# Each expert form's code split in two blocks: a short opening behind the comparisons and a rest reached by a hinted jump

## The chip, the cores and the metric

One core of one Trainium2 chip runs the kernel. The metric is the device time of one execution in microseconds (us). The profile takes one execution; it shows the engines PE (TensorE), its weight loads (PEld), DVE (VectorE), ACT (ScalarE), POOL (GpSimd) and SP (the engine that issues most transfers), and, under names with a q (PEldq, ACTq, DVEq), the instructions that an engine's sequencer handles itself: branches, register work, waits.

## The reference, cut to what matters

Two layers of a hybrid encoder: each has a token mixer, and after it a channel mixer, which is a dense SwiGLU in the first layer and a top-2-of-8 expert SwiGLU in the second. The expert part is what the change touches:

```
logits = t @ w_router + b_router              # t: 256 tokens x 1024
top_val, top_idx = top_k(logits, 2)
gates = softmax(top_val)
for each expert e, on the tokens routed to it:
    y_e = (silu(x @ w_gate_e[e]) * (x @ w_up_e[e])) @ w_down_e[e]     # 1024 -> 3584 -> 1024
out = sum over a token's two experts of gate * y_e
```

All is float32. An expert has 3 x 1024 x 3584 weights, 44 MB; the eight together are 352 MB of the 483 MB that the kernel reads.

## The kernel before

The program runs the mixer, the dense layer, the second mixer and the routing as straight code, and then a loop over the eight experts. How many tokens an expert gets is known only at run time (`cnt`), so each of PE, ACT and DVE holds the code of one expert six times, in six forms for up to 32, 64, 128, 160, 192 or 256 tokens (`NVAR`). POOL and SP run one loop body for all forms.

`experts(eng, name, emit)` (L618 to L649) writes this loop for one engine. A block `next` (L629, L630) adds one to the expert number and ends the loop after the eighth; `pick` (L632, L633) loads the token count from SBUF; a chain of comparisons (L641 for the forms under 128, L643 for those over it) jumps to the form. The six forms follow in the order 128, 32, 64, 160, 192, 256. Each begins with a branch hint (L646), which names the jump at the form's end (L648) and its target `next`. Only the form of 128 stands right behind the comparisons: the others lie behind it, 192 for instance some 7,500 PE instructions further on. A form's length in PE instructions is about 1,150 for 128, 2,360 for 32, 1,290 for 64, 2,670 for 160 and 2,440 for 192 (a matrix product of a rounded type is a weight load and a multiply, a float32 one two of each, and a transpose one of each).

An expert is 14 stages over the inner width. A stage takes two units of gate and up weights (halves of the 1024 rows, 1 MB each) and one unit of down weights. SP loads the units in order (L749) into a ring of 14 slots, and each of its loads waits until PE has finished with the slot's last unit, told by `gu_full` for a stage's gate and up product and by `down_done`.

- Forms 32 and 64 (`expert_whole`) multiply float32 directly. On PE, `gate_up(s)` (L1278) runs two stages ahead of `down(s)` (L1290); `turn` (L1264) transposes the activated product in between. ACT does `silu` of a stage, DVE the product `gated` (L2235) and a copy (L2257).
- Forms 128 and 256 (`expert_split`, L1388, L1419) and 160 and 192 (`expert_wide`, L1322, L1328, L1341, L1350) split each unit into a rounded high part (ACT, `weights_hi`, about 1.9 us) and a low part (DVE, `weights_lo`, L2241, about 2.3 us), and PE multiplies the parts. The inputs are split too (`h_parts`, DVE, L2268 and L2270, or L2311 and L2314).
- Before the first product of an expert PE waits for `xe` (the gathered tokens, copied by POOL, L2436, once the expert before has done its last gate and up product), and in the split forms for DVE's split of it and ACT's first high part.
- At an expert's end ACT and DVE copy the output from PSUM (`hT`), ACT issues its store, and all go back to `next`.

Of the kernel before, what the change touches and what calls it, by code (L numbers as in the profile page):

```python
# [281 lines left out]
def build(nc, ap, out, ypairs):  # L282
# [13 lines left out]
    with ExitStack() as ctx:  # L296
# [321 lines left out]
        def experts(eng, name, emit, first_variant=128):  # L618
# [25 lines left out]
            for n in sorted(NVAR, key=lambda n: n != first_variant):  # L644
                with nc.body(label(n), valid_engines=own):
                    back = eng.mark_branch_hint_location()  # L646
                    emit(eng.snap(turn, min_val=0, max_val=NE - 1), n)
                    eng.br(label("next")).branch_hint(back)  # L648
# [133 lines left out]
        def _(pe):  # L782
# [484 lines left out]
            def expert_whole(e, n):  # L1267

                def gate_up(s):

                    w = [landed_unit(e, "gu", s, h).rearrange("p (k c) -> p k c", k=KD // 2) for h in range(2)]
                    if s >= 2:
                        pe.wait_ge(act_ready, at_unit(e, n, s - 2))
                    bank = PG[:, s % 2, :]
                    width = gate_up_of(n, s)[3]
                    for k in range(KD):
                        for i in range(P // n):
                            last = mm(bank[i * n:(i + 1) * n, 0:width], xe[:, k, 0:n],  # L1278
                                      w[k // 4][:, k % 4, i * width:(i + 1) * width], start=(k == 0), stop=(k == KD - 1))
                    last.then_inc(gu_full, 2)  # L1280
# [12 lines left out]

                for i in range(STAGES + 2):
                    if i < STAGES:
                        gate_up(i)
# [12 lines left out]
            def expert_wide(e, n):  # L1309
# [54 lines left out]
                pe.wait_ge(x_split, e * 4 + 4)  # L1364
                for s in range(STAGES + 1):
                    if s < STAGES:
                        if s:
                            pe.wait_ge(act_ready, e * FT + FT + 2 * s - 1)
                        gate_up_half(s, 0)
# [8 lines left out]
            def expert_split(e, n):  # L1378
# [14 lines left out]

                def gate_up(s):
# [5 lines left out]
                    for h in range(2):  # L1400
                        q = expert_at["gu", s, h]
                        hi_ready(e, q)
                        if s == 0 and h == 0:
                            pe.wait_ge(x_split, e * 4 + 2)
                        gate_up_part(s, h, x_hi, w_hi_e[q % HI], opens=(h == 0))
                        if s == 0 and h == 0:
                            pe.wait_ge(x_split, e * 4 + 4)
                        gate_up_part(s, h, x_lo, w_hi_e[q % HI]).then_inc(hi_used, 1)
# [27 lines left out]

                for s in range(STAGES + 1):
# [8 lines left out]
            def expert(e, n):  # L1446
                pe.wait_ge(xe_ready, e + 1)
                (expert_whole if n < P else expert_split if n % P == 0 else expert_wide)(e, n)
# [18 lines left out]
        def _(act_e):  # L1467
# [224 lines left out]

            def silu(e, n, u, m):
# [22 lines left out]
            def expert_whole(e, n):  # L1716
                for u, s, j, m in units(n):
                    silu(e, n, u, m)
                ae.sem_inc(conv_hi, USES)
# [3 lines left out]
            def expert_wide(e, n):  # L1723
# [12 lines left out]
                for q in range(HI):  # L1736
                    weights_hi(e, q)
# [10 lines left out]
            def expert_split(e, n):  # L1748
                bl = turns(n)
                done = HI + 1  # L1750
                for q in range(done):
                    weights_hi(e, q)
# [13 lines left out]
            def expert(e, n):  # L1766
                (expert_whole if n < P else expert_split if n % P == 0 else expert_wide)(e, n)
# [28 lines left out]
        def _(ve):  # L1796
# [462 lines left out]
            def expert_whole(e, n):  # L2259
                for u, s, j, m in units(n):  # L2260
                    gated(e, n, u, m)
                    turned_whole(e, n, u, m)
                ve.sem_inc(conv_lo, USES)
                ve.sem_inc(x_split, 4)

            def expert_wide(e, n):
                ve.wait_ge(xe_ready, e + 1)
                V.tensor_copy(h_parts[:, 0, :, 0:n], xe[:, :, 0:n]).then_inc(x_split, 2)  # L2268
                ve.wait_ge(x_split, e * 4 + 2)
                V.tensor_tensor(h_parts[:, 1, :, 0:n], xe[:, :, 0:n], h_parts[:, 0, :, 0:n].bitcast(F32),  # L2270
                                ALU.subtract).then_inc(x_split, 2)
# [21 lines left out]
                for q in range(HI):  # L2293
                    weights_lo(e, q)
# [12 lines left out]
            def expert_split(e, n):  # L2307
                bl = turns(n)
                ve.wait_ge(xe_ready, e + 1)
                for i, j, m in bl:  # L2310
                    V.tensor_copy(x_hi[j], xe[:, :, j * P:(j + 1) * P]).then_inc(x_split, 2 // len(bl))  # L2311
                ve.wait_ge(x_split, e * 4 + 2)
                for i, j, m in bl:
                    V.tensor_tensor(x_lo[j], xe[:, :, j * P:(j + 1) * P], x_hi[j].bitcast(F32),  # L2314
                                    ALU.subtract).then_inc(x_split, 2 // len(bl))
                done = HI + 1
                for q in range(done):
                    weights_lo(e, q)
# [12 lines left out]
            def expert(e, n):  # L2331
                (expert_whole if n < P else expert_split if n % P == 0 else expert_wide)(e, n)
# [138 lines left out]
```

## Time and profile before

| | |
|---|---|
| three timed runs | 1830.52, 1839.72, 1842.34 us (median 1839.72) |
| the profiled execution's own time | 1832.89 us |
| its span, first to last instruction | 1831.1 us |
| mean granted TensorE clock | 0.917 of full |
| PE busy | 1598.6 us, 87% |
| DMA | 488.94 MB, mean 267 GB/s |

With the inputs used here the eight experts take the forms 32, 32, 128, 64, 160, 32, 192 and 64; they are called expert 0 to 7. They begin at about 822 us and end at about 1804 us of the span. A row of the chain of waits gives where the chain that ended last stood: start, length, and the engine and line that it stood on, "issue" being time in which the engine waited for nothing that the profile shows.

### The profile page before, as it was taken

How to read it: one execution, taken by the hardware profiler on the slowest of the kernel's cores; microseconds unless marked ns; L12 is line 12 of the kernel's file. 1: busy time of each engine (PE TensorE's matmuls, PEld its weight loads, DVE VectorE, ACT ScalarE, POOL GpSimd, SP SyncE). 2: the span in 40 equal slices, each digit the busy share in tenths (PEclk: the TensorE clock that was granted, in tenths of full speed). 3: DMA queues.
4: the chain of work that ended last, by engine and by line, in shares of the span. 5: the costliest groups of instructions: out<-in, count | busy, mean ns of one | idle time of the engine just before them, and what ended most of it. 6: DMA issues, size and time to landing. Idle time of an engine off the chain costs nothing.

```text
span 1831.1 us, 30902 instructions
## 1 busy us (share of the span) xinstructions
PE 1598.6 (87%) x12644; PEld 1288.1 (70%) x12645; DVE 710.6 (39%) x1017; ACT 545.7 (30%) x749; POOL 63.2 (3%) x66
## 2 busy tenths in 40 slices
PE   5999997999999999967566799989998749999894
PEld 4777776999987687746344687548897538888552
DVE  2162115555532431140000787116665015666212
ACT  2122114343321321020000676115654015545201
POOL 0010000000000100010000000000000000000002
PEclk8998598999999986898787899999999879999998
DMA  9632255744534133268999999999667997555794
GB/s 364 258 111 97 92 190 206 306 187 170 198 103 188 58 128 137 93 253 362 424 424 425 425 411 389 407 424 377 267 249 278 387 422 327 230 207 230 284 424 167
DMA packets 74563, 488.94 MB, mean 267 GB/s; under 512 B 9792, under 2 KB 13920, under 8 KB 16544
## 3 DMA queue, kind: packets, MB, share of 16 engines
q1 hardware_dynamic: 72176, 479.94, 65.2%
q10 hardware_dynamic: 1648, 4.59, 0.7%
q8 instruction: 119, 1.95, 0.4%
q0 software_dynamic: 576, 2.10, 0.4%
q14 instruction: 44, 0.36, 0.1%
HBM read 482.66 MB, written 3.93 MB: 266 GB/s over the span
## 4 chain that ended last, share of the span: by engine, by line
PE 78%; DMA 9%; issue 4%; DVE 4%; ACT 2%; POOL 1%; SPq 1%; ACTq 0%; POOLq 0%; DVEq 0%
PE PG L1278 9%; DMA arena<-in_experts 5%; PE Y L905 5%; PE PG L1388 4%; PE PG L1322 4%; PE TRB L1322 4%; PE Y L1290 4%; PE Y L1350 4%; PE Y L913 3%; PE Y L1162 3%; PE PG L869 3%; PE PG L870 3%; PE PG L871 3%; DMA ring<-in_experts 3%; PE TRB L1328 3%
## 5 line engine op out<-in xcount | busy, mean ns | idle before, releaser
L1278 PE MATMUL PG<-ring,mixT 128*32 128x128 f32 (+1 forms) x1920 | 115.2, 345 | 63.3 <-issue 63.3
L1471 ACT ACTIVATE parts<-ring 128x2048 fp32r<-128x2048 f32 x84 | 158.5, 1906 | 12.4 <-PE Y L871 8.2
L1278 PEld LDWEIGHTS PG<-ring,mixT 128*32 128x32 f32 (+1 forms) x1920 | 88.6, 136 | 93.6 <-issue 77.9
L2257 DVE COPY arena<-TRB 128x64 f32<-128x64 f32 (+1 forms) x70 | 17.6, 251 | 338.7 <-PE TRB L1264 338.7
L1471 ACT ACTIVATE rope<-PG 64x128 f32<-64x128 f32 (+2 forms) x84 | 27.1, 324 | 376.1 <-PE PG L1278 351.7
L1278 PE MATMUL PG<-arena,mixT 128*32 128x128 f32 (+1 forms) x1664 | 100.3, 349 | 41.7 <-issue 41.7
L869 PE MATMUL PG<-h_parts,parts 128*128 128x256 f32 x448 | 127.5, 285 | 10.2 <-DVE parts L2133 10.2
L870 PE MATMUL PG<-h_parts,parts 128*128 128x256 f32 x448 | 127.3, 284 | 0.0
L871 PE MATMUL PG<-h_parts,parts 128*128 128x256 f32 x448 | 127.1, 284 | 0.0
L1278 PEld LDWEIGHTS PG<-arena,mixT 128*32 128x32 f32 (+1 forms) x1664 | 78.1, 138 | 68.6 <-issue 55.5
L2133 DVE TENSOR_TENSOR parts<-ring,parts 128x2048 fp32r<-128x2048 f32 x42 | 95.9, 2292 | 25.6 <-ACT parts L1471 25.6
L2241 DVE TENSOR_TENSOR ring_parts<-ring,parts 128x2048 fp32r<-128x2048 f32 x42 | 95.0, 2287 | 20.8 <-PE Y L1341 18.4
L2241 DVE TENSOR_TENSOR parts<-arena,parts 128x2048 fp32r<-128x2048 f32 x42 | 95.2, 2287 | 18.3 <-PE Y L1341 15.5
L905 PE MATMUL Y<-hT,ring 128*128 128x256 f32 x416 | 93.6, 385 | 0.0
L869 PEld LDWEIGHTS PG<-h_parts,parts 128*128 128x128 f32 x448 | 85.6, 191 | 10.8 <-DVE parts L2133 10.4
L905 PEld LDWEIGHTS Y<-hT,ring 128*128 128x128 f32 x416 | 79.4, 193 | 11.2
L870 PEld LDWEIGHTS PG<-h_parts,parts 128*128 128x128 f32 x448 | 85.7, 191 | 0.0
L871 PEld LDWEIGHTS PG<-h_parts,parts 128*128 128x128 f32 x448 | 85.6, 191 | 0.0
L1471 ACT ACTIVATE parts<-arena 128x2048 fp32r<-128x2048 f32 x42 | 78.9, 1902 | 3.8 <-PE PG L1388 3.8
L913 PE MATMUL Y<-ring,hT 128*128 128x256 f32 (+2 forms) x320 | 63.5, 363 | 2.8 <-ACT hT L1471 2.8
L871 PE MATMUL Y<-parts 128*128 128x256 f32 x224 | 63.4, 283 | 0.0
L870 PE MATMUL Y<-parts 128*128 128x256 f32 x224 | 63.4, 283 | 0.0
(375 smaller groups left out, 2909.4 us busy)
## 6 DMA issues: line engine op xcount, KB each, us to landing
ring<-in_experts SPq DMA_DIRECT2D x168, 1024.0 KB, 13.0
arena<-in_experts SPq DMA_DIRECT2D x168, 1024.0 KB, 16.4
ring<-in_weights SPq DMA_DIRECT2D x116, 1024.0 KB, 5.8
ring<-in_weights SPq DMA_DIRECT2D x4, 512.0 KB, 4.1
ypairs<-hT ACTq DMA_DIRECT2D x3, 512.0 KB, 5.3
tok<-in_x SPq DMA_DIRECT2D x1, 1024.0 KB, 8.8
result<-scr SPq DMA_DIRECT2D x2, 512.0 KB, 2.6
ring<-in_weights SPq DMA_DIRECT2D x2, 432.0 KB, 6.7
```

Of the source, the lines that this page charges most:

```text
L869: mm(out_, w_hi[w][:, c], x[0], start=first, stop=False, skip_group_check=True)
L870: mm(out_, w_hi[w][:, c], x[1], start=False, stop=False, skip_group_check=True)
L871: return mm(out_, w_lo[w][:, c], x[0], start=False, stop=last, skip_group_check=True)
L905: last = mm(bank_part, ring[:, s, k, c:c + m], hT[:, k, :], start=(k == 0), stop=(k == KD - 1))
L913: last = mm(bank_part, hT[:, k, b * P:(b + 1) * P], ring[:, s, k, 0:m], start=(k == 0), stop=(k == KD - 1))
L1278: last = mm(bank[i * n:(i + 1) * n, 0:width], xe[:, k, 0:n], w[k // 4][:, k % 4, i * width:(i + 1) * width], start=(k == 0), stop=(k == KD ...
L1290: last = mm(o, actT[:, s % 2, f, 0:n], w[:, f, c:c + width], start=(s == 0 and f == 0), stop=(s == STAGES - 1 and f == 1))
L1322: last = mm(both, hi[:, k, i // 2, i % 2, :], h_parts[:, :, h * KD // 2 + k, 0:n], start=(h == 0 and k == 0), stop=False, skip_group_check ...
L1350: last = mm(o, a[:, s % 2, f, :], w[:, f, c:c + width], start=(opens and s == 0 and f == 0), stop=(closes and s == STAGES - 1 and f == 1))
L1471: return nc.scalar.activation(out_, in_, func, **kw)
L2133: V.tensor_tensor(w_lo[d % SPLITS], ring[:, slot_of[slot_of_dense(d)], :, :].rearrange("p k c -> p (k c)"), w_hi[d % SPLITS].bitcast(F32), ...
L2241: V.tensor_tensor(w_lo_e[q % SLOTS_E], ring_e[q % SLOTS_E].rearrange("p k c -> p (k c)"), w_hi_e[q % HI].bitcast(F32), ALU.subtract).then_ ...
```

## The change

Each form is written as two blocks instead of one. Six openings stand right behind the comparisons, in the old order; then come six rests in the same order. An opening ends in a jump to its rest, and a hint for this jump is the opening's first instruction; the rest begins with the hint for the jump back to `next`, as the whole form did. The functions that write an engine's part of an expert take a flag `opening` and write one piece or the other. What an opening holds:

- PE: the wait for `xe`; for 32 and 64 the half of stage 0's gate and up product that uses the first unit (16 and 8 of 32 and 16 products); for 128 and 256 the two high-part products of the first unit; for 160 and 192 all products of the first unit.
- ACT: `silu` of stage 0 (32 and 64), or the first three (160 and 192) or four (128 and 256) `weights_hi`.
- DVE: `gated` and the copy of stage 0 (32 and 64), or the split of `xe` and the first three or four `weights_lo`.

In the forms of 160 and 192 ACT gets a Silu of a single element at the head of the rest, ahead of the fourth `weights_hi`. Six openings take 46 instructions on ACT, 76 on DVE and about 300 on PE.

```diff
-            for n in sorted(NVAR, key=lambda n: n != first_variant):
+            layout = sorted(NVAR, key=lambda n: n != first_variant)
+            for n in layout:
                 with nc.body(label(n), valid_engines=own):
+                    on = eng.mark_branch_hint_location()
+                    emit(eng.snap(turn, min_val=0, max_val=NE - 1), n, True)
+                    eng.br(label(f"rest_{n}")).branch_hint(on)
+            for n in layout:
+                with nc.body(label(f"rest_{n}"), valid_engines=own):
                     back = eng.mark_branch_hint_location()
-                    emit(eng.snap(turn, min_val=0, max_val=NE - 1), n)
+                    emit(eng.snap(turn, min_val=0, max_val=NE - 1), n, False)
                     eng.br(label("next")).branch_hint(back)
...
+                if opening:
+                    gate_up(0, [0])
+                    return
                 for i in range(STAGES + 2):
                     if i < STAGES:
-                        gate_up(i)
+                        gate_up(i, [0, 1] if i else [1])
...
-                pe.wait_ge(x_split, e * 4 + 4)
+                if opening:
+                    pe.wait_ge(x_split, e * 4 + 4)
+                    gate_up_half(0, 0)
+                    return
...
-            def expert(e, n):
-                pe.wait_ge(xe_ready, e + 1)
-                (expert_whole if n < P else expert_split if n % P == 0 else expert_wide)(e, n)
+            def expert(e, n, opening):
+                if opening:
+                    pe.wait_ge(xe_ready, e + 1)
+                (expert_whole if n < P else expert_split if n % P == 0 else expert_wide)(e, n, opening)
...
+            def silu_table():
+
+                run(rc[0:1, 0, 0:1], rc[0:1, 0, 0:1], ACT.Silu)
...
-                for q in range(HI):
-                    weights_hi(e, q)
+                if opening:
+                    for q in range(HI):
+                        weights_hi(e, q)
+                    return
+                silu_table()
```

On PE, the form of 32 stood behind the whole form of 128; its first rows before (ISA rows are register work or a wait, L1278 the gate and up product, L1264 the transpose):

```order
L646 BRANCH_PREFETCH_HINT
L647 ISA
L1250 ISA
L1278 MATMUL PG<-ring,mixT 32x128 x64
L1255 ISA
```

And now, the openings of 128 and 32 (here L1403 is the product that was L1388, L1286 the one that was L1278), and then the head of the rest of 32:

```order
L643 COMPARE_AND_BRANCH x3
L647 BRANCH_PREFETCH_HINT
...
L649 UNCONDITIONAL_BRANCH
L647 BRANCH_PREFETCH_HINT
L648 ISA
L1256 ISA
L1286 MATMUL PG<-ring,mixT 32x128 x16
L649 UNCONDITIONAL_BRANCH
...
L652 BRANCH_PREFETCH_HINT
L653 ISA
L1286 MATMUL PG<-ring,mixT 32x128 x48
```

The first 16 of the 64 products moved up behind the comparisons, and a hint and a jump stand between them and the other 48.

On ACT, a wide form's head before, and after it the middle of its first stage's eviction (the `rope<-rope` row is the Silu):

```order
L646 BRANCH_PREFETCH_HINT
L647 ISA
L1471 ACT_TABLE_LOAD
L1471 ACTIVATE scr_parts<-ring 128x2048
L1471 ACTIVATE parts<-ring 128x2048 x2
L1705 ISA
...
L1731 REGISTER_ALU
L1471 ACT_TABLE_LOAD
L1471 ACTIVATE rope<-rope 128x2x192
```

And now, its opening and the head of its rest:

```order
L647 BRANCH_PREFETCH_HINT
L648 ISA
L1496 ACT_TABLE_LOAD
L1496 ACTIVATE scr_parts<-ring 128x2048
L1496 ACTIVATE parts<-ring 128x2048 x2
L649 UNCONDITIONAL_BRANCH
...
L652 BRANCH_PREFETCH_HINT
L1496 ACT_TABLE_LOAD
L1496 ACTIVATE rc<-rc 1x1
L1732 ISA
L1734 ISA
L1496 ACTIVATE scr_parts<-ring 128x2048
```

The first three copies moved up; the second table load stands ahead of the fourth copy instead of inside the eviction.

## Rows read from the trace of the kernel before

**Rows 1.** Windows of experts 1 and 5; the columns stand in its first row

```profile
core 0: us, PE busy (x) PEld busy (x) DVE busy (x) ACT busy (x) POOL busy (x), PEclk, DMA share, GB/s
899.00:1006.00 107.00, 61.48 (x1150) 46.40 (x1148) 8.12 (x30) 5.85 (x18) 1.95 (x2) 0.79 1.01 424
...
1405.00:1494.00 89.00, 59.69 (x1145) 45.93 (x1147) 12.30 (x34) 9.29 (x22) 2.04 (x2) 0.87 0.96 391
```

**Rows 2.** Chain of waits at expert 0's start: start, length, what

```profile
821.77 1.86 POOL mixT L2436
823.63 1.47 issue
825.10 6.39 PE PG L1278 x128
...
831.90 1.88 PE PG L1278 x64
```

**Rows 3.** Chain of waits at expert 5's start

```profile
1413.37 5.16 issue
1418.53 5.01 PE PG L1278 x128
```

**Rows 4.** Chain of waits at expert 6's start

```profile
1500.74 5.28 issue
...
1507.47 1.92 ACT scr_parts L1471
...
1509.43 1.65 PE PG L1322 x4
```

**Rows 5.** Chain of waits at expert 7's start, and a later stage's product

```profile
1712.55 5.90 issue
1718.45 8.63 PE PG L1278 x64
...
1727.73 3.60 PE PG L1278 x32
```

**Rows 6.** Jumps to a form on PE (ns, min/median/max), experts 0, 3, 5, 6, 7

```profile
L641 PEldq COMPARE_BRANCH  x1: 3352/3352/3352, 821.3 to 821.3; - x1
L641 PEldq COMPARE_BRANCH  x2: 67/212/357, 1142.2 to 1142.3; - x2
L641 PEldq COMPARE_BRANCH  x1: 4559/4559/4559, 1413.4 to 1413.4; - x1
L643 PEldq COMPARE_BRANCH  x2: 68/3178/6287, 1499.6 to 1499.7; - x2
L641 PEldq COMPARE_BRANCH  x2: 67/2634/5200, 1712.7 to 1712.8; - x2
```

**Rows 7.** All DMA queues, 1141 to 1144 us; then the instruction queues, 1499.6 to 1506.1

```profile
q1 hardware_dynamic: 177, 1.28, 100.9%
...
q8 instruction: 2, 0.03, 2.2%
q14 instruction: 2, 0.02, 0.7%
```

**Rows 8.** Windows behind the idle time: expert 5, then 7 (two); columns as rows 1

```profile
1418.50:1421.30 2.80, 2.77 (x56) 2.80 (x60) 0.00 (x0) 0.00 (x0) 0.00 (x0) 0.52 0.42 155
...
1718.40:1721.40 3.00, 2.95 (x14) 1.90 (x16) 0.00 (x0) 0.00 (x0) 0.00 (x0) 0.50 0.24 86
1721.40:1727.10 5.70, 5.70 (x53) 3.88 (x49) 0.43 (x1) 1.66 (x2) 0.00 (x0) 0.99 0.40 139
```

**Rows 9.** Jumps back to `next` on PE at the ends of experts 0 and 2

```profile
L648 PEldq COMPARE_BRANCH  x1: 3829/3829/3829, 901.9 to 901.9; - x1
...
L648 PEldq COMPARE_BRANCH  x1: 205/205/205, 1141.3 to 1141.3; - x1
```

**Rows 10.** Chain of waits at the start of expert 3

```profile
1141.20 3.03 PE Y L1419 x12
1144.23 5.97 PE PG L1278 x53
```

## What the change will do, predicted before it was run

> **What bounds the kernel now.** I read the chain of waits first, because the change moves only control flow: the question is where the chain stands still at an expert's start. It stands still at four of the eight, each time as "issue", time in which PE waits for no data: 1.47 us at expert 0 [rows 2], 5.16 us at expert 5 [rows 3], 5.28 us at expert 6 (there it is ACT that stands, and PE waits for ACT's first copy) [rows 4] and 5.90 us at expert 7 [rows 5]. That is 17.8 us, 1.0% of the span, and all that the openings can work on.
>
> The branch rows say what it is. A jump to a form costs PE 3352 to 6287 ns at experts 0, 5, 6 and 7, and 357 ns at expert 3 [rows 6]. While the dear ones last, blocks of instructions come in over DMA: two on the q8 queue (16 KB each, PE's) and two of 8 KB between 1499.6 and 1506.1 us, but none between 1141 and 1144 us, where expert 3's form is entered [rows 7]. So a jump is cheap when its target's block is still in the engine and dear when it must be fetched, and a fetch takes 3.35 us with the weight DMA idle and 4.6 to 6.3 us otherwise, partly because the block behind the comparisons is fetched first.
>
> Experts 1 and 5 are bound by DMA later on: shares of 1.01 and 0.96 at 424 and 391 GB/s, while PE is busy 61 of 107 us and 60 of 89 us [rows 1]. Expert 1 begins inside such a stretch, so its 3.8 us jump back [rows 9] and its jump to the form are covered by transfers, and I give its start nothing. In expert 5 the ring of weights is full when PE stands still, so the transfers begin again when stage 0 is done: what counts there is the end of stage 0.
>
> **Expert 6, the largest term.** ACT's opening for 192 stands 38 instructions behind `next`, in code that ACT has just run through. Its chain would go from 1500.74 to the table load after some 0.4 us instead of 5.28, so the first copy, 1507.47 to 1509.39, would end at 1504.5. DVE's split of the tokens starts at a jump that is equally near and is done by then. PE's opening for 192 lies some 200 instructions behind `next`, and I take it to lie in the next 16 KB block, the first of the two fetched in PE's 6.29 us. One fetch cost 3.35 us at the least [rows 6]: 1499.7 + 3.35 = 1503.1, and if it took 5 us, 1504.7. PE starts at 1504.5 instead of 1509.43: 4.9 us. Bounds: 3.5 (the block lands as late as 1505.9) and 5.1 us. I take **4.8**. The rest's block has the whole opening to come in: 32 products, and the low half waits for DVE until 1506.8 at least.
>
> **Expert 5.** Now: jump at 1413.42, 4.56 us, first product at 1418.53. [...] After: jump 0.4, entry 0.55 as now, start at 1414.4; 32 products at 1.88/64 us [rows 2] take 0.94 us, to 1415.3. [...] Gain 1.2 to 1.9, I take **1.6**.
>
> **Expert 7.** Now: jump at 1712.78, 5.20 us, first product at 1718.45, 14 in 3.0 us at a clock of 0.50, then about 0.11 us each [rows 5, 8]: stage 0's 32 end at 1723.4. After: start at 1713.7, 16 products at 3.60/32 us take 1.8, to 1715.5. The rest is there at 1713.2 + 5.2 = 1718.4, PE goes on at 1718.6 and needs 1.8 or, at 14 in 3.0 us, 3.4 us: 1720.4 to 1722.0. Gain 1.4 to 3.0, I take **2.2**.
>
> **Expert 0.** POOL's copy of `xe` ends at 821.77 + 1.86 = 823.63, and PE starts 1.47 us later, since its 3.35 us fetch began at 821.26 [rows 2, 6]. After, PE waits in its opening and starts about 0.25 us behind the copy, 1.2 us earlier. Its first 32 products take 1.6 us (128 in 6.39 us [rows 2]), to 825.5, and the rest's block, asked for at 821.7, is there at 825.1. I take **1.2**.
>
> **Costs.** Eight more hints and jumps on each engine. A jump whose block is there costs 0.2 to 0.36 us [rows 6, 9]. At expert 3 PE's products follow one another without a gap, 1141.20 + 3.03 = 1144.23 [rows 10], while the sequencer branches: what was issued ahead hides it; without that cover it would be 0.4 us. At experts 2 and 4 PE waits for ACT, which runs through its old order. I charge **0.5** in all. The moved table load, the same length as before, leaves the first eviction of the wide forms and is paid ahead of the fourth copy; PE still has queued products in both places, so I give it nothing (1.28 us twice at most, either way).
>
> Sum: 4.8 + 1.6 + 2.2 + 1.2 - 0.5 = **9.3 us**. Against the profiled execution, 1832.9, that is 1823.6. That execution stands 6.8 us under the median of the timed runs; the four together (1830.5, 1832.9, 1839.7, 1842.3) have a mean of 1836.4, and I forecast from it: 1827.
>
> [...] Expert 3's form was entered in 357 ns with no block coming in, though it lies 3,500 instructions behind `next`; it shares a block with the end of the form of 32, last run 130 us before, so PE keeps more than two blocks. [...]
>
> **Rivals.**
> A. *The hint fetches nothing when its jump stands in the same block.* For: every hint of today stands far ahead of its jump, and expert 0's jump back still took 3.8 us [rows 9]; a hint's block seems to be asked for only as PE enters the block that holds the jump. Then the rest is asked for when the sequencer gets to the jump. At expert 0 that is 824.2, behind the wait for `xe`: PE goes on at 827.7 and stage 0 ends 0.9 us later than now instead of 1.2 earlier. Expert 5 keeps 0.9, expert 7 1.6, expert 6 4.3: 5.4 us, 1831. Against: nothing in these rows.
> B. *The gain is partly taken by the ring.* Expert 5's and 0's gains end in stretches bound by transfers [rows 1]; if these do not start earlier by as much, 6.5 us stay: 1830.
> C. *Slower: every second jump is a full miss.* The rest pays 6.3 us, the dearest of [rows 6], from its jump on, at all starts on the chain. Expert 0: -3.4; expert 3, free today, -4.6 (6.3 less 1.7 of opening); expert 5: -1.0; expert 6: +0.6, its second half product starting at 1515.3; expert 7: +0.8. Sum 7.6 us slower: 1844. It decides from about 5 us for the second jump. Against: fetches of 3.35 and 4.56 us are in the rows, and part of the 6.29 is the first block, which is then already there.
> D. *More.* With an idle time of 3 us instead of 5 the clock may hold its upper level at experts 5 and 7, all upper bounds hold, and the table load leaves the chain: 1.9 + 3.0 + 5.1 + 1.2 + 1.3 = 12.5 us, 1824.
>
> **How the numbers follow.** Forecast (7.5 to 11.5 us) 0.45; A 0.22; B 0.10; C 0.08; D 0.15. Range: from D less the scatter of the executions around their mean (6 us), 1817, to A and B plus as much but short of C's far end, 1840. A change of 1% is 18 us, about what a measurement of this kernel can tell from none; no case reaches it alone, only with scatter: faster 0.08, same 0.89, slower 0.03.
>
> **What would show it.** In the profile after: expert 6's first product about 7 us behind the end of expert 5's last, not 12; the jumps of L641 and L643 on PE under 0.5 us except towards 160, 192 and 256; new jump rows at the openings' ends, of 1 to 3.5 us at experts 5 and 7 by the forecast, over 3 us at expert 0 by A, over 5 us by C; expert 3's start still without a gap. The forecast is wrong if ACT's opening is not in its store, so that the 5.28 us stay, or if expert 3 or 4 gets a new wait.

## The result, and the profile after

The changed kernel is slower: 1859.28 us median (1856.73, 1856.87, 1861.70, 1862.83) against 1838.30 for the kernel before beside it (four runs, 1830.52 to 1842.34). The ratio is 1.0122, 95% interval 1.0094 to 1.0149, some 22 us. The forecast was 1827 us and the range ended at 1840; a slowdown of over 1% had a chance of 0.03.

| | before | after |
|---|---|---|
| profiled execution's span, us | 1831.1 | 1859.9 |
| PE busy, us | 1598.6 | 1617.8 |
| mean granted TensorE clock | 0.917 | 0.907 |
| instruction blocks fetched, q8 (PE) / q14 | 119 / 44 | 121 / 49 |

Where the time arises is read from POOL's copies of `xe`, one at each expert's start. The timeline of POOL, kernel after (start, length, line, out<-in, and in brackets POOL's idle time before):

```profile
828.73 1.89 POOL L2482 COPY mixT<-arena 128x2048 f32 x1 [28.14 <-issue]
911.44 1.90 POOL L2482 COPY mixT<-arena 128x2048 f32 x1 [80.82 <-PE PG L1286]
```

The other six start at 1016.12, 1147.82, 1233.60, 1421.53, 1514.04 and 1727.74 us. Before, the same copies start at 821.73, 898.94, 1005.88, 1137.33, 1223.02, 1404.69, 1493.55 and 1703.66. The first is 7.0 us later after, and nothing ahead of it was changed. That part is scatter of one execution: the run with all forms whole (below) has its first copy at 829.24 too, and its ratio is 0.999. The other 21.8 us arise within the experts. From copy to copy (the last to the end of the span) the eight experts are longer by 5.5, -2.3, 0.3, 0.1, 6.3, 3.7, 3.6 and 4.7 us. A figure for one expert carries scatter too: the run with all forms whole differs from before by 1.8 us at expert 0 and by -1.6 at expert 1.

The chain of waits at expert 0's start, after, answers to [rows 2]:

```profile
830.63 0.13 issue
830.76 1.94 PE PG L1286 x32
832.70 2.14 issue
834.84 4.15 PE PG L1286 x96
...
839.64 6.27 issue
845.92 0.04 DVEq L652
```

PE starts 0.13 us behind the copy, where it was 1.47. Then the chain stands still twice, 2.14 us for the rest of PE's form and 6.27 us for the rest of DVE's. The same at expert 5 [rows 3] and expert 7 [rows 5]:

```profile
1430.06 0.74 issue
1430.79 1.08 PE PG L1286 x32
1431.87 5.93 issue
1437.81 4.73 PE PG L1286 x96
...
1443.15 5.86 issue
1449.01 0.04 DVEq L652
```

```profile
1736.63 0.80 issue
1737.43 0.64 PE PG L1286 x2
...
1740.97 3.22 issue
1744.19 7.09 PE PG L1286 x48
...
1752.11 5.47 issue
```

So the early start was had, 0.7 to 0.8 us in place of 5.2 and 5.9, and given back with more on top. In the kernel before, DVE's fetch ran beside PE's, in idle time: PE's jump to the form lasts from 1413.42 to 1417.98 us, and DVE's sequencer stands behind its own from 1414.91 to 1420.70 us. The 128 products of [rows 3] end at 1423.54 us in the trace and DVE's next product starts at 1424.06, 0.5 us behind:

```profile
1424.06 0.30 DVE rope L2235
```

Now the same 128 end at 1442.54 and DVE's product starts at 1449.26, 6.7 us behind.

The products behind this stall also run at a lower granted clock. Ten microseconds from the next transposes of expert 5 on, before and then after (columns as in [rows 1]):

```profile
1424.50:1434.50 10.00, 9.28 (x235) 7.33 (x235) 1.56 (x6) 0.81 (x3) 0.00 (x0) 1.00 1.00 417
```

```profile
1449.70:1459.70 10.00, 10.00 (x178) 7.38 (x182) 1.40 (x6) 0.54 (x2) 0.00 (x0) 0.71 0.85 324
```

PE gets through 178 instructions at a mean clock of 0.71, where it got through 235 at 1.00. It had been busy for only 1.9 of the 6.7 us of the stall, and the clock stands at 0.50 from 1448.6 to 1455.4 us. Over the whole of expert 5 PE is busy 64.1 us instead of 59.6, over expert 0 55.3 instead of 52.4. How much of this counts in the time is not shown: later parts of both experts are bound by the weight transfers (a DMA share of 1.01 at 424 GB/s from 860 to 911 us and from 1460 to 1508 us).

Expert 6, after [rows 4]:

```profile
1521.22 1.28 ACT L1496
...
1528.08 2.92 PE PG L1335 x8
...
1535.56 3.58 issue
```

ACT no longer stands for 5.28 us ahead of its table load. But PE is not ready until 1528.1: its jump to the opening starts at 1523.0 and lasts 4.61 us (below). And at 1535.56 it waits 3.58 us for the rest. The start of expert 4 has a wait that was not there at all. Chain of waits:

```profile
1240.39 0.09 DVE hT L2385
1240.48 5.54 issue
1246.02 0.04 DVEq L629
```

It is DVE's jump back to `next` (L629 is the instruction in it). A second wait of 3.47 us stands inside DVE's opening, at 1247.35 us; its cause is not shown. Expert 3's start has no gap, as in [rows 10]: the last product of the one before ends at 1154.71 us and the first of expert 3 starts there.

The jumps on PE answer to [rows 6, 9]. By line, after: opening to rest (L649) at experts 0, 1, 3, 5, 6 and 7 (expert 2's takes 3.46 us), then to the openings of 160 and 192 (L643), then back to `next` (L654) behind experts 3 and 5 (behind 0 and 1 5.29 and 5.54 us, before 3.83 and 2.01; experts 1 and 2, which begin there, did not get clearly longer).

```profile
L649 PEldq COMPARE_BRANCH  x1: 3370/3370/3370, 831.2 to 831.2; - x1
L649 PEldq COMPARE_BRANCH  x1: 6112/6112/6112, 921.5 to 921.5; - x1
L649 PEldq COMPARE_BRANCH  x1: 324/324/324, 1154.7 to 1154.7; - x1
L649 PEldq COMPARE_BRANCH  x1: 6484/6484/6484, 1431.1 to 1431.1; - x1
L649 PEldq COMPARE_BRANCH  x1: 6123/6123/6123, 1532.7 to 1532.7; - x1
L649 PEldq COMPARE_BRANCH  x1: 4824/4824/4824, 1739.1 to 1739.1; - x1
...
L643 PEldq COMPARE_BRANCH  x3: 65/67/4307, 1242.1 to 1242.3; - x3
L643 PEldq COMPARE_BRANCH  x1: 4611/4611/4611, 1523.0 to 1523.0; - x1
...
L654 PEldq COMPARE_BRANCH  x1: 3850/3850/3850, 1237.2 to 1237.2; - x1
L654 PEldq COMPARE_BRANCH  x1: 5501/5501/5501, 1516.3 to 1516.3; - x1
```

Behind experts 3 and 5, before:

```profile
L648 PEldq COMPARE_BRANCH  x1: 419/419/419, 1226.6 to 1226.6; - x1
...
L648 PEldq COMPARE_BRANCH  x1: 2736/2736/2736, 1495.8 to 1495.8; - x1
```

The DMA view between the hint and the jump at expert 0 (828.5 to 831.2 us), and then while the jump lasts (831.2 to 834.6 us): PE's queue q8 carries nothing ahead of the jump.

```profile
q14 instruction: 1, 0.01, 1.1%
...
q8 instruction: 1, 0.02, 2.4%
```

### The profile page after: what moved, and what is told of

It is laid out like the page before. It is cut to its first block, busy times and chain, and to the rows that moved or that the text cites. A ratio compares the mean times of both kernels' runs of the same rounds, so it can differ in the third digit from the quotient of the medians.

```text
span 1859.9 us, 30968 instructions
## 1 busy us (share of the span) xinstructions
PE 1617.8 (87%) x12644; PEld 1296.6 (70%) x12645; DVE 710.8 (38%) x1017; ACT 545.9 (29%) x751; POOL 63.1 (3%) x66
## 4 chain that ended last, share of the span: by engine, by line
PE 78%; DMA 8%; issue 6%; DVE 4%; ACT 2%; POOL 1%; SPq 1%; ACTq 0%; DVEq 0%; POOLq 0%
PE PG L1286 8%; PE Y L911 5%; DMA arena<-in_experts 5%; PE PG L1335 4%; PE Y L1300 4%; PE TRB L1335 4%; PE PG L1403 4%; PE Y L1363 4%; PE Y L919 3%; PE Y L1168 3%; PE PG L875 3%; PE PG L876 3%; PE PG L877 3%; PE TRB L1341 3%; PE PG L1341 3%
## 5 line engine op out<-in xcount | busy, mean ns | idle before, releaser
L1286 PE MATMUL PG<-ring,mixT 128*32 128x128 f32 (+1 forms) x1920 | 119.7, 354 | 56.7 <-issue 52.3
L1286 PEld LDWEIGHTS PG<-ring,mixT 128*32 128x32 f32 (+1 forms) x1920 | 89.7, 140 | 89.9 <-issue 72.8
L1286 PE MATMUL PG<-arena,mixT 128*32 128x128 f32 (+1 forms) x1664 | 102.1, 352 | 39.1 <-issue 39.1
L1286 PEld LDWEIGHTS PG<-arena,mixT 128*32 128x32 f32 (+1 forms) x1664 | 78.8, 139 | 68.0 <-issue 54.6
L2279 DVE TENSOR_TENSOR ring_parts<-ring,parts 128x2048 fp32r<-128x2048 f32 x42 | 95.0, 2288 | 21.5 <-PE Y L1354 19.0
L2279 DVE TENSOR_TENSOR parts<-arena,parts 128x2048 fp32r<-128x2048 f32 x42 | 95.2, 2288 | 17.3 <-PE Y L1354 14.7
L1335 PE MATMUL PG<-h_parts,scr_parts 128*128 128x320 f32 (+1 forms) x224 | 45.7, 348 | 23.8 <-DVE h_parts L2311 13.2
L1335 PEld LDWEIGHTS PG<-h_parts,scr_parts 128*128 128x128 f32 x224 | 37.3, 198 | 41.0 <-issue 20.7
## 6 DMA issues: line engine op xcount, KB each, us to landing
arena<-in_experts SPq DMA_DIRECT2D x168, 1024.0 KB, 14.7
```

The source lines that it names most:

```text
L1286: last = mm(bank[i * n:(i + 1) * n, 0:width], xe[:, k, 0:n], w[k // 4][:, k % 4, i * width:(i + 1) * width], start=(k == 0), stop=(k == KD ...
L1335: last = mm(both, hi[:, k, i // 2, i % 2, :], h_parts[:, :, h * KD // 2 + k, 0:n], start=(h == 0 and k == 0), stop=False, skip_group_check ...
L2279: V.tensor_tensor(w_lo_e[q % SLOTS_E], ring_e[q % SLOTS_E].rearrange("p k c -> p (k c)"), w_hi_e[q % HI].bitcast(F32), ALU.subtract).then_ ...
```

## The experiments

**The theory, before the runs.** (1) A hint whose jump stands in the same block of instructions fetches nothing, so each rest is fetched only when its jump is reached. On ACT and DVE the openings end behind waits for data, so their fetches now follow one behind the other on the chain. (2) The new layout moves borders of blocks, and with them the jumps back that miss (3.85 us on PE behind expert 3, 0.42 before). Rivals: PE's second jump alone costs it; the moved table load; scatter. The expected effects were worked out from the delta by expert above.

All twelve, the ratio being to the kernel before on the same chip, with its 95% interval; "sum" is the eight experts in the profiled execution against before's:

| run | what | ratio | sum, us |
|---|---|---|---|
| after | the change | 1.0122 (1.0094 to 1.0149) | +21.8 |
| 1 | after, no opening hints | 1.0100 (1.0064 to 1.0135) | +22.0 |
| 2 | all forms whole | 0.9993 (0.9966 to 1.0019) | -0.7 |
| 3 | openings on PE alone | 1.0048 (1.0021 to 1.0075) | +8.3 |
| 4 | openings on ACT and DVE alone | 1.0069 (1.0043 to 1.0096) | +14.7 |
| 5 | as 4, no data wait in the whole forms' openings | 1.0032 (1.0009 to 1.0054) | +2.2 |
| 6 | as 4, rest of 64 ahead of rest of 32 | 1.0028 (1.0007 to 1.0049) | +4.7 |
| 7 | whole forms, comparisons at each end | 0.9978 (0.9952 to 1.0004) | -1.9 |
| 8 | as 7, early hints | 0.9934 (0.9906 to 0.9962) | -12.5 |
| 9 | as 3, hint a block ahead of its jump | 1.0052 (1.0034 to 1.0069) | +6.6 |
| 10 | as 8, PE's form of 192 moved by 101 instructions | 0.9917 (0.9885 to 0.9949) | -13.9 |
| 11 | as 8, hints on PE alone | 0.9935 (0.9907 to 0.9963) | -8.4 |
| 12 | 5 and 6 together | 1.0011 (0.9990 to 1.0033) | +3.4 |

### 1. Without the hints

```diff
                 with nc.body(label(n), valid_engines=own):
-                    on = eng.mark_branch_hint_location()
                     emit(eng.snap(turn, min_val=0, max_val=NE - 1), n, True)
-                    eng.br(label(f"rest_{n}")).branch_hint(on)
+                    eng.br(label(f"rest_{n}"))
```

> The changed kernel without the hints of the six openings (the jump to each rest stays). Theory 1 (a hint whose jump stands in the same block of instructions fetches nothing, so the rest is fetched only when its jump is reached): the time is that of the changed kernel, ratio to before 1.012 plus or minus 0.003, and PE's second jumps still take 3.4 us at expert 0 and 6.1 to 6.5 us at experts 1, 5 and 6. Rival (the hints do fetch, only too late): each second jump gets longer by what the hint had hidden, 1 us or more at seven places, and the time rises by 3 us or more over the changed kernel.

Measured 1856.81 us, 1.0100, against the changed kernel's 1.0122; the intervals overlap widely. PE's second jumps take 3.63, 5.98 and 6.75 us at experts 0, 1 and 5, where the hinted ones took 3.37, 6.11 and 6.48. On PE the hints gained nothing that the rows show: each second jump changed by at most 0.7 us, some up and some down.

### 2 to 4. Taken apart by engine

In the function that lays out the forms, with `split` false, true for PE, or true for ACT and DVE (the rest blocks are then laid out for the split engines only):

```diff
+            split = name in ()          # run 3: ("pe",); run 4: ("act", "dve")
             for n in layout:
                 with nc.body(label(n), valid_engines=own):
+                    if not split:
+                        back = eng.mark_branch_hint_location()
+                        e = eng.snap(turn, min_val=0, max_val=NE - 1)
+                        emit(e, n, True)
+                        emit(e, n, False)
+                        eng.br(label("next")).branch_hint(back)
```

> The changed kernel's code order (the table load of the wide forms moved, the first half product apart) but each form in one block again, as before. Theory 1 and theory 2 (what costs is the second jump, or the borders of the blocks that move with it) both expect the time of the kernel before, ratio 1.000 plus or minus 0.003. A rival that blames the moved table load or scatter of the runs expects some of the 1.2% to stay: 1.003 to 1.012.

1833.18 us, 0.9993. The new order of the code, the table load with it, costs nothing that can be told from none: the loss comes with the split into two blocks.

> Openings on PE alone; ACT's and DVE's forms stand in one block each. Theory 1: PE's own second jump costs about 3 us at expert 0 and about as much as it gains at experts 5 and 7, PE's jump back to the comparisons misses as in the changed kernel, and the chain ACT miss, DVE miss behind it is gone: 0 to 6 us over before, ratio 1.000 to 1.004. Rival (PE's second jump is what costs, as rival C of the prediction had it): 12 us or more over before, ratio over 1.007.

1841.99 us, 1.0048: 0.0048 x 1837 = 8.8 us, a little over what I expected of it and under the rival's 12. By expert +0.9, 0.8, -0.8, -1.4, 3.0, 0.9, 4.1, 0.7: the early starts at experts 0, 5 and 7 just pay for the second jump, and experts 4 and 6 lose. There PE's jump back takes 6.06 and 5.51 us, 0.42 and 2.74 before, and the opening's own block must be fetched too (4.47 and 4.53 us).

> Openings on ACT and DVE alone; PE's forms stand in one block each. Theory 1: ACT's miss of 2.6 to 5.3 us and DVE's of 5.5 to 6.3 us follow one another at experts 0, 5, 6 and 7, where before they ran beside PE's own: 8 to 16 us over before, ratio 1.004 to 1.009, with ACT's opening of expert 6 the only gain (about 4 us). Rival (PE's second jump is what costs): within 4 us of before, ratio 1.000 plus or minus 0.002.

1849.03 us, 1.0069, 12.7 us. By expert +4.0, -1.9, -1.2, 0.9, 8.5, 0.4, 0.2, 3.8. The rival is out. Runs 3 and 4 add up to 21.5 us, what the change cost. At expert 6 the gain on ACT that I expected did not show. PE's jump to its form takes 6.45 us as before (6.29), which would leave about 3 us, but PE's jump back ahead of it took 5.50 us instead of 2.74.

In this run the chain stands at expert 0's stage 0, and at expert 4's start:

```profile
837.87 5.72 issue
...
1237.34 5.52 issue
```

Both are DVE's: the first is its second jump, the second its jump back.

### 5, 6 and 12. The two costs of ACT's and DVE's openings

Run 5:

```diff
                     if split:
                         on = eng.mark_branch_hint_location()
-                        emit(eng.snap(turn, min_val=0, max_val=NE - 1), n, True)
+                        if n >= P:
+                            emit(eng.snap(turn, min_val=0, max_val=NE - 1), n, True)
                         eng.br(label(f"rest_{n}")).branch_hint(on)
...
                 with nc.body(label(f"rest_{n}"), valid_engines=own):
+                    e = eng.snap(turn, min_val=0, max_val=NE - 1)
+                    if n < P:
+                        emit(e, n, True)
```

> Like the run with openings on ACT and DVE alone, but for the forms below 128 tokens the openings there hold only the jump, so that no wait for data stands between the two jumps. Theory 1 (what costs at experts 0, 5 and 7 is that ACT's and DVE's fetches start only behind a wait for data, and so one behind the other): the 4.0 us of expert 0 and 3.8 us of expert 7 go, expert 4's 8.5 us stay; 6 to 9 us under that run, ratio to before 1.002 to 1.004. Rival (each further jump costs its fetch wherever it stands): the time of that run, 1.007.

1840.99 us, 1.0032. Expert 0's 4.0 us fell to 0.2, expert 7's 3.8 to 1.6; expert 4 kept 6.0 of 8.5. In the chain DVE's miss behind stage 0 is gone: PE's products run from 831.16 to 837.46 and the next transposes follow at once. The fetches themselves have not gone: DVE's sequencer stands 2.9, 5.8 and 5.3 us at its second jump at experts 0, 5 and 7, now beside PE's fetch (3.67, 4.72 and 5.34 us). The edit also moves instructions from the openings to the rests, and so borders of blocks; that this did the gain is unlikely, as the fetches are all still there, but no run separates it.

Run 6:

```diff
-            for n in layout if split else []:
+            for n in ([128, 64, 32] + layout[3:]) if split else []:
                 with nc.body(label(f"rest_{n}"), valid_engines=own):
```

> Like the run with openings on ACT and DVE alone, with the rest of 64 laid out ahead of the rest of 32. [...] Rival (form 160's opening itself costs the 8.5 us): expert 4 stays 7 us or more over before.

1843.60 us, 1.0028. Expert 4's 8.5 us fell to 2.5, and both engines went on from their jump back behind expert 3 within 0.3 us (5.1 us on ACT and 5.6 on DVE in run 4). The rival is out: most of that cost hangs on where the blocks lie and not on what is in them. I found no jump back of ACT or DVE with a miss behind form 32's experts (0, 1, 5 and 7) either. That the order of two blocks decides whether this jump back must fetch is shown; by what rule it does is not.

> Openings on ACT and DVE alone with both repairs: no wait for data between the two jumps in the forms below 128 tokens, and the rest of 64 laid out ahead of the rest of 32. If the two causes found (misses behind a wait, 7 us; a border that makes the jump back behind expert 3 miss, 7 us) are separate and are all of the 12.7 us, they add up: nothing of the loss is left and the early start of ACT at expert 6 (about 3 us) shows: ratio to before 0.997 to 1.000, expert 4's start within 2.5 us of before, experts 0 and 7 within 2. If a third cost is there, 1.001 or more stay.

1841.76 us, 1.0011 (0.9990 to 1.0033). The two repairs take 10.7 of the 12.7 us and mostly add up. Experts 0 and 7 came to -0.2 and -0.6 and expert 4 to 2.3, as expected, but expert 6 did not gain; it stands at +2.0. The chain of waits there shows why, both stalls being DVE's:

```profile
1506.96 4.95 issue
...
1513.00 4.17 issue
```

The first is its jump back behind expert 5, a form of 32. The second stands right behind the hint at the head of the opening of 192; run 6 has 4.29 us at the jump to that opening. So in this layout DVE's jump back does miss behind one of form 32's four experts, where run 6 had no such miss. In the time as a whole the 2 us that are left can't be told from none.

### 7 and 8. The next form known early

The row count of expert e + 1 is read in expert e, and every form ends in its own comparisons. In run 8 one of seven hints is set there, by the next form:

```diff
                 with nc.body(label(n), valid_engines=own):
+                    emit(e, n, True)
+                    eng.reg_add(coming, turn, 1)
+                    eng.br_lt(coming, NE, on_true=label(f"look_{n}"), on_false=label(f"on_{n}_done"))
+                with nc.body(label(f"look_{n}"), valid_engines=own):
+                    e1 = eng.snap(coming, min_val=1, max_val=NE - 1)
+                    eng.reg_load(rows, cnt[0:1, bass.ds(e1, 1)])
+                    eng.br(label(f"look_{n}_tree"))
+                choose(f"look_{n}_", f"on_{n}_")       # run 7: straight to rest_{n}
+                for k in layout + ["done"]:
+                    with nc.body(label(f"on_{n}_{k}"), valid_engines=own):
+                        marks[k] = eng.mark_branch_hint_location()
+                        eng.br(label(f"rest_{n}"))
+                with nc.body(label(f"rest_{n}"), valid_engines=own):
+                    emit(e, n, False)
+                    eng.reg_add(turn, turn, 1)
+                    eng.br_lt(turn, NE, on_true=label(f"tail_{n}_tree"), on_false=label(f"go_{n}_done"))
+                choose(f"tail_{n}_", f"go_{n}_")
+                for k in layout + ["done"]:
+                    with nc.body(label(f"go_{n}_{k}"), valid_engines=own):
+                        eng.br(label(k)).branch_hint(marks[k])
```

`choose` writes the old comparisons, with jumps to the blocks of the second name. The rest of a form follows its opening without a gap. On ACT and DVE the forms of 32 and 64 look ahead before their first instruction.

> Forms whole again, and every form has its own copy of the count's load and the comparisons at its end, so that there is no jump back and no block of shared comparisons to fetch first; the count of the next expert is read ahead. Theory (the dear jumps of 6.3 us are two fetches one behind the other): the jumps to the forms of experts 1 and 6 fall from 6.3 to 3.5 to 5 us on PE, those of 5 and 7 stay near 4.6 to 5; 0 to 6 us under before, ratio 0.997 to 1.000. If a jump costs as before, 1.000 to 1.002, for the added comparisons.

1834.27 us, 0.9978 (0.9952 to 1.0004). Without hints the jumps to the forms of experts 1 and 6 stayed at 5.8 and 6.1 us: I was wrong that they would fall. Two blocks come in there too, at 1505.50 and at 1510.46 us for expert 6, around a jump that starts at 1506.87; the first is, I take it, the one behind the form's last block. The jump to expert 3's form, 0.36 us before, now took 6.02. The jumps to the forms of experts 5 and 7 fell to 3.9 and 3.8.

> Like the run with comparisons at each form's end, and the form of the next expert is looked up near the start of the present one, where one of seven hints is set for the jump at the end, so that a border of blocks lies between hint and jump wherever the form is long enough. Theory 1 (a hint fetches its target when the block that holds the jump is entered): the jumps to the forms of experts 5, 6 and 7 take under 1 us on PE, and 10 to 16 us go against before, ratio 0.991 to 0.995. Rival (hints fetch nothing in this program): the time of the run without them plus 1 us for each of 8 chains of comparisons, 1.000 to 1.005.

1825.34 us, 0.9934 (0.9906 to 0.9962), 12 us faster. On PE the jumps to the forms of experts 1 to 6 take under 0.5 us, and q8 carries 110 blocks instead of 117. ACT and DVE stand still at no form's start behind the first. By expert 1.1, 1.0, -1.3, -1.0, 0.0, -3.2, -6.1, -3.1. Hints do fetch, then. One jump stayed dear, that to expert 7.

PE's jumps to the forms of experts 1, 2, 3, 5 and 6 take 3.9 to 6.1 us without the hints (run 7) and 0.3 to 0.4 us with them (run 8).

### 9. A hint one block ahead of its jump

On PE, the hint of each opening moved between comparisons and openings, and 256 waits and a jump that are never run put behind it (`gap` is the target of a comparison that never goes that way):

```diff
+            for n in layout:
+                with nc.body(label(f"on_{n}"), valid_engines=own):
+                    marks[n] = eng.mark_branch_hint_location()
+                    eng.br(label(n))
+            with nc.body(label("gap"), valid_engines=own):
+                for _ in range(256):
+                    eng.wait_ge(xe_ready, 1)
+                eng.br(label("done"))
             for n in layout:
                 with nc.body(label(n), valid_engines=own):
-                    on = eng.mark_branch_hint_location()
                     emit(eng.snap(turn, min_val=0, max_val=NE - 1), n, True)
-                    eng.br(label(f"rest_{n}")).branch_hint(on)
+                    eng.br(label(f"rest_{n}")).branch_hint(marks[n])
```

> Like the run with openings on PE alone, but each opening's hint is set right behind the comparisons and 129 instructions that are never run stand between these and the openings, so that the openings of 128, 32, 64 and 160 lie in the 256-instruction block behind the one that holds hint and comparisons. Theory 1 (a hint fetches its target when the block that holds the jump is entered): the packet of the rest's block starts before the second jump and not 0.6 us behind it; PE's second jump falls from 3.4 us to at most 1.2 at expert 0, and by 1 us or more from 6.1 and 6.5 at experts 1 and 5. The first jumps can get dearer (3 to 5 us), so the time as a whole may stay or grow: ratio 1.000 to 1.007. Rival (hints for a jump this near never fetch): second jumps as in the run on PE alone.

The trace bears out the counts of 129 and of 256 instructions. In the kernel before, a block of 16 KB comes in on q8 every 256 instructions of PE, in the mean of the 38 steps ahead of the experts. In the form of 160 (expert 4) PE's blocks come in 92 to 188 instructions earlier in the form than in run 3, 129 in the mean of nine.

Jump from opening to rest at experts 0, 1 and 5, by line (3.29, 6.15 and 6.50 us in run 3):

```profile
L667 PEldq COMPARE_BRANCH  x1: 1146/1146/1146, 828.6 to 828.6; - x1
L667 PEldq COMPARE_BRANCH  x1: 5061/5061/5061, 915.2 to 915.2; - x1
L667 PEldq COMPARE_BRANCH  x1: 4523/4523/4523, 1420.8 to 1420.8; - x1
```

The DMA view of 826.2 to 828.6 us, between hint and jump, shows the block of PE that was missing there in the changed kernel:

```profile
q14 instruction: 3, 0.02, 3.2%
q8 instruction: 1, 0.02, 2.6%
```

All three fell as said, though at expert 0 the hint stands only some 2.5 us ahead. So it was not nearness in time that made the old hint idle. That a border of blocks must lie between hint and jump fits; by this run alone, the number of instructions between them could be it as well (run 10 settles that). At experts 1 and 5 the jump comes only 0.8 and 0.6 us behind the entry into the opening, and 1.1 and 2.0 us are gained. The time as a whole did not gain (1844.76 us, 1.0052): the first jumps now cost 2.4 to 4.5 us at experts 1, 2, 4, 5, 6 and 7.

### 10 and 11. The dear jump, and which engine

Run 10 puts 200 waits and a jump that are never run ahead of PE's form of 192 in run 8, in the way of run 9, 101 instructions by my count. In that form PE's blocks come in 51 to 143 instructions earlier than in run 8, 104 in the mean of nine.

> The run with comparisons and early hints at each form, with 101 instructions that are never run ahead of PE's form of 192. In that run the jump from 192 to 64 cost 3.30 us in spite of its hint. Theory (its jump stood within a few instructions of a border of blocks, so that its block was entered only just before it): moved to a third of a block behind the border the jump takes under 0.5 us, expert 7 starts about 3 us earlier, the rest stays: ratio 0.990 to 0.993. Rival (the hint from 192 is lost for another reason): the jump stays over 3 us, 0.9934.

My count of instructions put the jump out of 192 within a dozen of a border of blocks; no view shows the count. The jump to expert 7's form on PE, run 8 and then run 10, and the chain of waits there in the same order:

```profile
L677 PEldq COMPARE_BRANCH  x1: 3296/3296/3296, 1702.2 to 1702.2; - x1
```

```profile
L685 PEldq COMPARE_BRANCH  x1: 325/325/325, 1706.0 to 1706.0; - x1
```

```profile
1701.19 1.20 PE Y L1388 x4
1702.38 3.35 issue
1705.73 0.42 PE PG L1311
```

```profile
1705.20 1.21 PE Y L1396 x4
1706.42 0.03 issue
```

When PE's blocks came in bears the count out. In run 8 none comes between 1689 us and the jump at 1702.18, and the next starts at 1703.08. In run 10 one comes at 1692.28, 13.7 us ahead of the jump; the DMA view of 1689 to 1706 us has it:

```profile
q8 instruction: 1, 0.02, 0.3%
```

In both runs the hint stands a whole form ahead of its jump, so the distance between them is not what decides.

The fetch is gone: expert 7 is 6.4 us shorter than before, where run 8 had 3.1. The time is 1823.10 us, 0.9917 (0.9885 to 0.9949), the best of all and 15 us under the kernel before; against run 8 alone the intervals overlap.

> Comparisons at each form's end on all three engines, early hints on PE alone. If PE's fetches are what stands on the chain, this has nearly the whole gain, 0.993 to 0.995; if ACT's and DVE's fetches (2.6 to 5.9 us each, beside PE's in the kernel before) take their place once PE's are gone, 2 to 6 us of the 12 are lost: 0.995 to 0.998.

1827.30 us, 0.9935 (0.9907 to 0.9963): the gain of run 8 within its interval. The profile shows one fetch of ACT that takes PE's place, 6.5 us at expert 5, which is as long as before where run 8 had gained 3.2; experts 6 and 7 are within 1 us of run 8. PE's fetches are most of it.

## Why the prediction was wrong

- **Where the kernel stood still** was right. The 17.8 us of idle starts were real, and runs 8 and 10 took back 12 and 15 us.
- **The openings start early** was right on the rows: 0.13, 0.74 and 0.80 us in place of 1.47, 5.16 and 5.90, and ACT's 5.28 us at expert 6 gone. Expert 3 enters without a gap, as its row had it before.
- **"The rest is there at 1713.2 + 5.2 = 1718.4"** failed at expert 7, where the jump to the rest still took 4.82 us, and so did the same step at expert 0 (3.37 us). Rival A had named the mechanism (0.22); runs 1, 9 and 10 show it. Its price, 5.4 us faster in all, was still of the wrong sign: PE's openings alone cost 8.8 us (run 3).
- **Expert 5, 1.6 us.** No run shows the gain of 1.2 to 1.9 us that this term stands on. The runs showed a loss, 0.9 us in run 3 and 3.7 in the changed kernel. The jump to the rest took 6.48 us, where the jump to the form had taken 4.56. It starts at 1431.05 us and the one block of PE that begins to come in while it lasts does so at 1435.18 us, so it was not under way when the jump came; the weight DMA runs beside it (a share of 0.73 from 1431.0 to 1437.6 us).
- **"Costs. Eight more hints and jumps on each engine"**, charged 0.5 us in all, is the step that decided: the split of ACT's and DVE's forms costs 12.7 of the 21.5 us that runs 3 and 4 add up to. I followed second jumps on PE only. ACT's and DVE's fetches had run beside PE's, ahead of the first data (at expert 5 DVE's ended at 1420.70 us and ACT's at 1422.18, the first products at 1423.54). Put behind an opening that ends in a wait for data, DVE's is 5.5 to 6.3 us on the chain at experts 0, 5 and 7. Run 5 takes back 6.8 of the 12.7 us by moving that wait. In rival C, too, only PE's jumps were priced.
- **Jumps back** were given no term. Behind expert 3 they now miss on all three engines (3.85 us on PE, where it was 0.42, 5.3 on ACT and 5.6 on DVE). Run 6 ties those of ACT and DVE to the layout. Behind expert 5 PE's takes 5.50 instead of 2.74, and what sets that is open: run 4, with PE's forms whole, has 5.50 too, and runs 2, 5, 6 and 12, whole as well, have 1.2 to 2.5.
- **The clock behind a stall** was no term of the sum either. Rival D let it hold its upper level at the starts of experts 5 and 7; behind the new stall it fell, as the rows of expert 5 show (0.71 where it was 1.00). What this term is worth is not shown.
- **Expert 6, 4.8 us**: ACT was priced right. PE's fetch of its opening was too, at 3.35 to 5 us: it took 4.61; but the jump back ahead of it cost 2.8 more than before. PE's first product comes 10.5 us behind expert 5's last (1517.58 to 1528.08), not 7. "The rest's block has the whole opening to come in" failed with the hint: 3.58 us of wait. The upper bound, 5.1 us, also lay above the 4.9 that the prediction's own time of ACT's copy allows.
- **Rival C's total** (1844, chance 0.08) had the sign at a third of the size. Its 7.6 us are near the 8.8 of PE's openings alone, by luck: it had them at experts 0, 3 and 5, and run 3 has them at 4 and 6. The range's end at 1840 left no room for a cost on the engines that I had not followed.

## What to carry to other kernels

Here, splitting code to bring its first part near moved a fetch from where engines wait anyway to where they wait for one another: DVE's 5.5 to 6.3 us came onto the chain at experts 0, 5 and 7. Before it is done, list for every engine (not only the busiest) what stands between the first jump and the second: with a wait for data there the fetch stood on the chain, and without it 6.8 of 12.7 us came back (run 5). In this kernel a hint worked only with a border of blocks between it and its jump (1.15 us at expert 0 in run 9, 3.29 in run 3), and took the whole fetch away only where a long stretch of the form lay between that border and the jump (0.3 us at expert 7 in run 10, 3.3 in run 8). Where the target depends on data, read the data early, choose among several hints, and give each place its own copy of the comparisons.

## What the runs showed of the hardware

- The runs fit a branch hint that acts when the block that holds its jump is entered. With no border between, those of PE's second jumps that must fetch take 2.6 to 6.5 us with it (the changed kernel and run 3) and 2.8 to 6.8 without it (run 1). With one between (run 9) expert 0's takes 1.1 us, with the weight DMA idle (a share of 0.03), and those of experts 1 and 5 5.1 and 4.5 us, 1.1 and 2.0 less than in run 3; expert 2's takes 4.1 us, 1.6 more. In run 8, where the hints stand early in the form, the jumps to experts 1 to 6 take 0.2 to 0.4 us.
- A miss on ACT or DVE does not show in its branch row (52 and 65 ns in the changed kernel at jumps to a rest that then stood for 2.6 to 5.3 us on ACT and 5.5 to 6.3 us on DVE); it is the gap to the next instruction of that engine's sequencer. On PE the row holds it.
- Instructions that never run saved 3 us: with 101 of them, by my count, one jump went from 3.30 to 0.33 us (runs 8 and 10).
- PE's granted clock was 0.71 in the 10 us behind a stall of 6.7 us in which PE was busy for 1.9, where it was 1.00 without the stall.
- Not settled: what makes the jump back of ACT and DVE behind expert 3 miss in the one layout (5.1 and 5.6 us, run 4) and not in the other (0.3 us, run 6), PE's jump back behind expert 5 (1.2 to 5.5 us with its forms whole), and the first expert's fetch (3.5 and 3.3 us on PE in runs 8 and 10), which no run hinted.
